# Two output projections of a two-block kernel, from single-precision matmuls to products of high and low parts

## The reference

```python
def first_block(...):
    for layer in range(DEPTH):
        x = x + FFN_HALF * swiglu(rms_norm(x, norm_g[layer, 0]), ffn_w13[layer, 0], ffn_w2[layer, 0])
        h = rms_norm(x, norm_g[layer, 1])
        if layer < N_A_LAYERS:
            y_mix, q_mem = short_conv_mixer(h, conv_w_in[layer], conv_w[layer])
        else:
            ...
            y_mix = causal_mla_attention(q_nope, q_rope, k_nope, k_rope, v)
        y_mem = memory_attention(q_mem, mem, mem_norm_g[layer], w_mem_kv[layer], g_mem_q[layer], g_mem_k[layer])
        x = x + jnp.concatenate([y_mix, y_mem], axis=-1) @ w_out[layer]
        x = x + FFN_HALF * swiglu(rms_norm(x, norm_g[layer, 2]), ffn_w13[layer, 1], ffn_w2[layer, 1])
```

## Time and profile before

| | us |
|---|---|
| median of 3 runs | 3403.96 |
| lowest to highest | 3402.34 to 3404.91 |
| the profiled execution | 3403.58 |
| its span, first to last instruction | 3401.8 |
| mean granted TensorE clock | 0.981 |
| out0 on TensorE | 322.6 to 350.5 |
| out1 on TensorE | 960.0 to 990.9 |

### The profile page before, as it was taken

How to read it: one execution, slowest core, us unless ns; L and a number is a source line. 1 busy time by engine, 2 the same in 40 slices (tenths; PEclk the granted TensorE clock), 3 DMA queues, 4 the chain that set the end, 5 groups by cost and what they waited for, 6 DMA issues and landing times.

```text
span 3401.8 us, 51940 instructions
## 1 busy us (share of the span) xinstructions
PE 3274.9 (96%) x20178; PEld 2934.0 (86%) x20178; DVE 1975.3 (58%) x2057; ACT 1623.6 (48%) x1916; POOL 1248.1 (37%) x507
## 2 busy tenths in 40 slices
PE   7999999999799999999999999997999999999998
PEld 7998999998479989898999898986788888888886
DVE  4544644644434464252443471616888888888887
ACT  4343434332233344531443355403777777777775
POOL 6764787870038855250886353400000000000000
PEclk9999999999699999999999999998999999999999
DMA  5443444543124433344444433344988988988986
GB/s 221 168 160 127 170 180 160 185 176 133 50 101 184 173 137 138 123 161 149 174 184 162 160 126 147 137 149 172 354 332 330 368 329 328 369 329 329 367 330 245
DMA packets 97078, 707.31 MB, mean 208 GB/s; under 512 B 10784, under 2 KB 10784, under 8 KB 10944
## 3 DMA queue, kind: packets, MB, share of 16 engines
q1 hardware_dynamic: 96768, 704.42, 55.5%
q10 hardware_dynamic: 144, 1.05, 0.1%
q0 software_dynamic: 48, 0.13, 0.0%
HBM read 704.51 MB, written 1.05 MB: 207 GB/s over the span
## 4 chain that ended last, share of the span: by engine, by line
PE 84%; DVE 5%; issue 4%; POOL 3%; DMA 2%; ACT 2%; DVEq 0%; POOLq 0%; ACTq 0%; SPq 0%
PE bank L578 20%; PE bank L579 20%; PE bank L580 20%; PE bank L667 10%; POOL half_lo L540 3%; DVE kept L2095 2%; PE bank L664 2%; PE bank L957 2%; DMA ring<-experts 2%; PE bank L1087 1%; PE bank L761 1%; PE bank L1104 1%; PE bank L635 1%; PE bank L783 1%; PE bank L1131 1%
## 5 line engine op out<-in xcount | busy, mean ns | idle before, releaser
L540 POOL TENSOR_TENSOR half_lo<-ring,half_hi 128x1024 fp32r<-128x1024 f32 x502 | 1247.2, 2491 | 967.4 <-ACT half_hi L1213 964.0
L1213 ACT ACTIVATE half_hi<-ring 128x1024 fp32r<-128x1024 f32 x502 | 528.8, 1060 | 759.8 <-PE bank L580 651.3
L578 PE MATMUL bank<-h_hi,half_hi 128*128 128x256 f32 x2928 | 839.1, 287 | 11.2 <-POOL half_lo L540 8.4
L579 PE MATMUL bank<-h_lo,half_hi 128*128 128x256 f32 x2928 | 830.8, 284 | 0.0
L580 PE MATMUL bank<-h_hi,half_lo 128*128 128x256 f32 x2928 | 830.8, 284 | 0.0
L1625 ACT ACTIVATE expert_parts<-ring 128x1024 fp32r<-128x1024 f32 x672 | 674.7, 1054 | 282.5 <-DMA ring<-experts 224.6
L578 PEld LDWEIGHTS bank<-h_hi,half_hi 128*128 128x128 f32 x2928 | 563.5, 192 | 17.5 <-POOL half_lo L540 6.6
L2289 DVE TENSOR_TENSOR expert_parts<-ring,expert_parts 128x1024 fp32r<-128x1024 f32 x448 | 527.6, 1222 | 74.5 <-ACT expert_parts L1625 72.9
L579 PEld LDWEIGHTS bank<-h_lo,half_hi 128*128 128x128 f32 x2928 | 563.4, 192 | 0.7
L580 PEld LDWEIGHTS bank<-h_hi,half_lo 128*128 128x128 f32 x2928 | 563.2, 192 | 0.0
L578 PE MATMUL bank<-expert_parts,h_hi 128*128 128x512 f32 x896 | 360.0, 402 | 11.6 <-DVE kept L2276 6.9
(11 more groups left out here) (299 smaller groups left out, 4397.6 us busy)
## 6 DMA issues: line engine op xcount, KB each, us to landing
ring<-experts SPq DMA_DIRECT2D x336, 1024.0 KB, 4.8
ring<-stream SPq DMA_DIRECT2D x330, 1024.0 KB, 4.8
con<-consts SPq DMA_DIRECT2D x1, 1473.0 KB, 8.2
kept<-x_in SPq DMA_DIRECT2D x1, 1024.0 KB, 4.8
kept<-mem SPq DMA_DIRECT2D x1, 1024.0 KB, 16.3
lent<-mem SPq DMA_DIRECT2D x1, 1024.0 KB, 18.3
lent<-mem ACTq DMA_DIRECT2D x1, 1024.0 KB, 8.0
out<-kept SPq DMA_DIRECT2D x1, 1024.0 KB, 3.9
```

The lines of the kernel that those rows point to most:

```text
L540: nc.gpsimd.tensor_tensor(half_lo[:, h % HALVES, :], ring[:, u % RING, s * HALF:(s + 1) * HALF], half_hi[:, h % HALVES, :].bitcast(F32), A ...
L578: mm(dst, w_hi, x_hi, start=start, stop=False, skip_group_check=shared)
L579: mm(dst, w_hi, x_lo, start=False, stop=False, skip_group_check=shared)
L1213: nc.scalar.activation(half_hi[:, h % HALVES, :], ring[:, u % RING, s * HALF:(s + 1) * HALF], ACT.Copy).then_inc(hi_ready, 1)
```

## The change

out0 and out1 become split units too (`is_parted`), and a new function `parted` on TensorE multiplies them: three fp32r products for each tile, as elsewhere, over each half's four tiles of input channels, both output halves accumulating over the two halves of the unit. Their inputs are no longer one f32 page: VectorE writes each head's result and the gated convolution twice, as a high part (a copy to fp32r) and a low part (the subtraction of the high part). For out0, TensorE's first half waits only for the first two pairs of the convolution (`conv_part`), its second half for everything (`y_ready`). ScalarE makes the halves of out0 and out1 through the same `feed`, and `opening_by_units` now runs `done` for each of the four units.

```diff
--- before
+++ after
@@ -87,6 +87,11 @@
     return name[:3] == "ffn" or name in ("conv_in", "mla_in") or name[:2] in ("xq", "gx", "ax", "ay", "gr", "mu", "mo", "gm")
 
 
+def is_parted(name):
+
+    return is_split(name) or name in ("out0", "out1")
+
+
 def layer_order(l):
 
     runs = [("kv", 0, 8) if l else ("kv", 6, 2), ("mu", 0, 4), ("xq", 0, 4), ("ax", 0, 4), ("gx", 0, 4), ("wv", 0, 1), ("ay", 0, 1),
@@ -121,7 +126,7 @@
         STREAM.append(START[name] + j)
         UNIT_OF.append(name)
 
-SPLIT = [is_split(name) for name in UNIT_OF]
+SPLIT = [is_parted(name) for name in UNIT_OF]
 RANK = [sum(SPLIT[:u]) for u in range(DENSE_UNITS + 1)]
 SPLIT_UNITS = [u for u in range(DENSE_UNITS) if SPLIT[u]]
 
@@ -439,7 +445,6 @@
         mem_raw, mem_n = page(3), (page(5), page(9))
         rs_x, rs_m, rs_xx = rs[:, 4 * TOK:5 * TOK], rs[:, 3 * TOK:4 * TOK], rs[:, 5 * TOK:6 * TOK]
         mem_k, mem_v, mem_q = page(10)[:, 4:6, :], page(10)[:, 6:8, :], page(11)[:, 6:8, :]
-        Y_conv, Y_mla = page(5), page(7)
         gate_c, conv_u, conv_y = page(6, CT), padded(7, CT, 2), page(8, CT)
         k_nope, k_rot, k_rope = page(8)[:, 0:6, :], page(8)[:, 6:7, :], page(8)[:, 7:8, :]
         v_mla = tokens(11, MLA_HEADS * VHD)
@@ -449,6 +454,17 @@
         q_rope, q_rot = page(3)[:, 0:3, :], page(3)[:, 3:6, :]
         rs_flat, sg_flat = rs, sg[:, :, :].rearrange("p a b -> p (a b)")
         mem2 = page(4)
+        def part(i):
+
+            return expert_parts[:, lent_pages.index(i), 0:KT * TOK].rearrange("p (k t) -> p k t", k=KT)
+
+        mem_parts = [hid_hi[:, i, j * TOK:(j + 1) * TOK] for i in range(2) for j in range(2)]
+        conv_hi = [part(5)[:, k, :] for k in range(CT)] + mem_parts[0:2]
+        conv_lo = [part(11)[:, k, :] for k in range(CT)] + mem_parts[2:4]
+        mla_hi = [part(10)[:, k, :] for k in range(6)] + mem_parts[0:2]
+        mla_lo = [hid_lo[:, i, j * TOK:(j + 1) * TOK] for i in range(2) for j in range(2)] \
+            + [part(10)[:, k, :] for k in (6, 7)] + mem_parts[2:4]
+
         xk, xv, xq, gx = page(5), tokens(6, D), page(8), page(10)
         yx, merged = xq, gx
         ax, ay, gr = padded(9, KT, 3), page(7), page(3)
@@ -591,6 +607,26 @@
                         last = products(b[:, m * 256:m * 256 + 256], w_hi[:, cols], w_lo[:, cols], h_hi[:, k, :],
                                         h_lo[:, k, :], k == 0, k == KT - 1)
                     last.then_inc(first_done if m == 0 else unit_done, 1)
+
+            def parted(b, u, x_hi, x_lo, token_major, ready=None):
+
+                for s in range(2):
+                    w_hi, w_lo = half(u, s)
+                    if ready:
+                        ready[s]()
+                    for m in range(2):
+                        dst = b[:, m * 256:(m + 1) * 256]
+                        for i in range(4):
+                            k = 4 * s + i
+                            start, stop = s == 0 and m == 0 and i == 0, s == 1 and i == 3
+                            if token_major:
+                                toks, cols = slice(m * PARTS, (m + 1) * PARTS), slice(i * 256, (i + 1) * 256)
+                                last = products(dst, x_hi[k][:, toks], x_lo[k][:, toks], w_hi[:, cols], w_lo[:, cols],
+                                                start, stop, True)
+                            else:
+                                cols = slice(i * 256 + m * PARTS, i * 256 + (m + 1) * PARTS)
+                                last = products(dst, w_hi[:, cols], w_lo[:, cols], x_hi[k], x_lo[k], start, stop, True)
+                    last.then_inc(first_done if s == 0 else unit_done, 1)
 
             def column_half(b, u, m):
 
@@ -646,13 +682,16 @@
                 opening(*pairs)
                 project(None, units[2:])
 
-            def project(src, units, token_major=False, fresh=False):
+            def project(src, units, token_major=False, fresh=False, parts=None, ready=None):
 
                 for u in units:
                     p = SLOT[u]
                     b = bank[p % 3]
 
                     wait(pe, bank_read[p % 3], p // 3)
+                    if parts:
+                        parted(b, u, parts[0], parts[1], token_major, ready if u == units[0] else None)
+                        continue
                     if SPLIT[u]:
                         split_columns(b, u, 0, fresh and u == units[0])
                         continue
@@ -845,8 +884,9 @@
                           lambda h: project(None, conv[6:7] if h == 0 else []),
                           lambda: project(None, conv[4:5]))
 
-            pe.wait_ge(y_ready, t.add("y", 1))
-            project(Y_conv, AT["out0"])
+            y_all = t.add("y", 1)
+            project(None, AT["out0"], parts=(conv_hi, conv_lo),
+                    ready=(lambda: pe.wait_ge(conv_part, 2), lambda: pe.wait_ge(y_ready, y_all)))
             ffn(AT["ffn01"][0], D_FF // 256)
 
             ffn(AT["ffn10"][0], D_FF // 256, lambda: norm(KT, KT, ones))
@@ -910,7 +950,7 @@
                       lambda h: [(q_nope[:, h, :], k_nope[:, h, :]), (MEM_HALF(q_rot, h), k_rot[64 * (h % 2):64 * (h % 2) + 64, 0, :])],
                       lambda h, j, m: v_mla[:, m, h * VHD:(h + 1) * VHD], 1, VHD)
             pe.wait_ge(y_ready, t.now("y"))
-            project(Y_mla, AT["out1"])
+            project(None, AT["out1"], parts=(mla_hi, mla_lo))
             ffn(AT["ffn11"][0], D_FF // 256)
 
 
@@ -1273,10 +1313,12 @@
                 for j in range(4):
                     x_square(j)
 
-            def opening_by_units(g, u0):
+            def opening_by_units(g, u0, units=None):
 
                 for j in range(4):
-                    if j == 3:
+                    if units:
+                        done(units[j])
+                    elif j == 3:
                         feed(2 * RANK[u0], u0 - 1 + RING)
                     x_high(g, j)
                     x_square(j)
@@ -1390,7 +1432,7 @@
             act.wait_ge(sin_in, 1)
             nc.scalar.activation(angle[:, 1:3, :], angle[:, 1:3, :], ACT.Sin).then_inc(sin_ready, 1)
             t.add("x", 1)
-            opening_by_units(gain("norm_g", 2), AT["ffn01"][0])
+            opening_by_units(gain("norm_g", 2), AT["ffn01"][0], AT["out0"])
             ffn_x(AT["ffn01"][0], D_FF // 256)
             def mem2_squares():
                 act.wait_ge(mem_loaded, 16)
@@ -1470,7 +1512,7 @@
             attention(MEM_HEADS, lambda h: value_out(kv, 1) if h == 0 else None, lambda: value_out(kv, 0))
             attention(MLA_HEADS)
             t.add("x", 1)
-            opening_by_units(gain("norm_g", 5), AT["ffn11"][0])
+            opening_by_units(gain("norm_g", 5), AT["ffn11"][0], AT["out1"])
             ffn_x(AT["ffn11"][0], D_FF // 256)
 
             for l in range(2):
@@ -1904,9 +1946,18 @@
                     last.then_inc(normed, 1)
                     t.add("norm", 1)
 
-            def mem_attention(Y, early=None, between=None):
-                attention(MEM_HEADS, MEM_HD ** -0.5, None, lambda h: v.tensor_copy(
-                    MEM_HALF(Y[:, CT:, :], h), bank[7][64 * (h % 2):64 * (h % 2) + 64, 0:TOK]), early, between)
+            def put_parts(got, hi, lo):
+
+                did(v.tensor_copy(hi, got))
+                return v.tensor_tensor(lo, got, hi.bitcast(F32), ALU.subtract)
+
+            def mem_attention(early=None, between=None):
+
+                def put(h):
+                    r = slice(64 * (h % 2), 64 * (h % 2) + 64)
+                    return put_parts(bank[7][r, 0:TOK], mem_parts[h // 2][r, :], mem_parts[2 + h // 2][r, :])
+
+                attention(MEM_HEADS, MEM_HD ** -0.5, None, put, early, between)
 
 
             def lam_start():
@@ -1966,8 +2017,12 @@
 
                 q = SLOT[conv[7 + j]]
                 dve.wait_ge(unit_done, conv[7 + j] + 1)
-                v.tensor_tensor(Y_conv[:, 2 * j:2 * j + 2, :], two(bank[q % 3]), conv_y[:, 2 * j:2 * j + 2, :],
-                                ALU.mult).then_inc(bank_read[q % 3], 1)
+                pair = slice(2 * j, 2 * j + 2)
+                v.tensor_tensor(conv_y[:, pair, :], two(bank[q % 3]), conv_y[:, pair, :], ALU.mult).then_inc(bank_read[q % 3], 1)
+                wait_read(dve, q)
+                did(v.tensor_copy(part(5)[:, pair, :], conv_y[:, pair, :]))
+                v.tensor_tensor(part(11)[:, pair, :], conv_y[:, pair, :], part(5)[:, pair, :].bitcast(F32), ALU.subtract)\
+                 .then_inc(conv_part, 1)
 
             def beside_head(h):
                 if h == 0:
@@ -1982,7 +2037,7 @@
                 if h == 3:
                     gate_b(1)
 
-            mem_attention(Y_conv, lambda: conv_in(0), beside_head)
+            mem_attention(lambda: conv_in(0), beside_head)
             gate_b(2)
 
             tick(y_ready)
@@ -2062,10 +2117,10 @@
                 else:
                     norm_piece(q_rope, 2 * i - 6, 5 - i, P("g_q_rope"), sg_flat, i == 4)
 
```

(5 more changed lines are left out.)

## The result

| us | before | after |
|---|---|---|
| median (15 runs each) | 3404.82 | 3412.20 |
| lowest to highest | 3401.28 to 3413.94 | 3404.72 to 3426.96 |
| the profiled execution | 3403.58 | 3404.72 |
| its span | 3401.8 | 3402.9 |
| ratio after/before, 95% interval | | 1.0026 [1.0017, 1.0034] |

The kernel became slower by 0.26%, about 8.8 us (5.8 to 11.6). The forecast was 3415 in a range of 3402 to 3421, with 0.71 on slower.

What follows compares the result with a forecast made beforehand. TensorE, busy 96% of the span, and whatever leaves it waiting were taken to set the time. First projection +0.8 us and second +10.8 made +11.6 on 3403.58, 0.4 below the median: 3415, range 3402 to 3421.

Steps and rivals of the forecast that it cites:

- rival A: Loads don't hold ScalarE on the path, taking away 10.4 us and 2.9 of clock terms: 3402 us; chance 0.13.
- B: Rival: a clean gain, neither loads nor GpSimd hold anything, -7.6 us: 3396 us; chance 0.07.
- D: Rival: the three products take as long as the f32 one: 3424 us; chance 0.10 together with C.
- C: Rival: low clock through one more MLA head or longer into out1, +3 to +5 us: 3419; 0.10 with D.
- products of out0, out1: Each of eight units goes from 6.92 to 5.76 us on TensorE: 4.6 us less per projection.
- `gate_b(0)` beside head 2: GpSimd holds VectorE's added cast and subtraction, so head 3's transposes start 3.7 us later; 1.9 by the median row.
- clock behind it: After TensorE's idle time beside `gate_b(0)` the clock falls: 1.7 us more, bounds 0 and 3.5.
- squares of the queries: Before the query norms, ScalarE's out1[0] copies wait for a load behind kv0[3]: 6.3 us later, bounds 2.0 and 9.5.
- first norm round: After 8.4 us idle, the first query norm round runs at half clock, 2.09 for 1.13 us: 0.9 more.
- first `at_t`: In head 0, ScalarE's out1[1] copy waits for a load behind kv0[4]: 4.1 us later, bounds 1.1 and 8.
- kv0[5]: Behind head 0's values, kv0[5] runs at the lower clock: 2.0 us more, bounds 0 and 3.5.
- puts in memory attention, MLA: Each head's copy gets a second VectorE instruction: 0.9 us in the second memory attention, 0.9 in MLA.

Runs made afterwards that it cites:

- e2: Changed kernel with only the first projection (out0) split, the second as before: 3403.24 us, 0.9995 of before.
- e3: Changed kernel with only the second projection (out1) split, the first as before: 3413.59 us, 1.0024 of before.
- e4: Changed kernel, but ScalarE makes out1's first halves later, beside MLA heads 4 and 5: 3400.12 us, 0.9991 of before.
- e7: Changed kernel with both the edits of e5 and e6, later convolution parts and late out1 halves: 3394.83 us, 0.9981 of before.
- e5: Changed kernel, but VectorE makes the gated convolution's parts later, the first pair's beside head 3: 3408.97 us, 1.0018 of before.
- e8: Kernel before plus only two ScalarE waits for out1's loads, behind the read-outs of kv0[3] and kv0[4]: 3412.34 us, 1.0030 of before.
- e1: Changed kernel run again without edit, for a second profile: 3410.80 us, 1.0021 of before.
- e6: As e4, but out1's first half is made beside MLA head 0 and the other two beside head 5: 3397.16 us, 0.9985 of before.

## Why the prediction was right

**The cause.** The forecast rested on ScalarE's copies waiting in order for loads that cannot start before kv0[3] and kv0[4] are done. It is shown from three sides: the loss lies in out1 (e2, e3), it goes when the copies stand elsewhere (e4 -10.7, e7 against e5 -14.1, where the forecast's rival A takes 13.3 away), and it comes without the rest of the change (e8). Rivals A and B fall with this, and D with the 5.67 us of a unit. C, a low clock through one more head, is in neither profile: in after and e1 the clock was back one MLA head earlier than in the profile of before, worth about 3 us, and e8, which has before's products and copies, shows that earlier return too (e2 shows before's later one). The slowest executions, up to 3426.96 us, have no profile, so there C isn't excluded.

**The terms,** as forecast and as the profile of after has them, us:

| term | forecast | after |
|---|---|---|
| products of out0, out1 | -4.6, -4.6 | -4.6, -5.0 |
| start of out0 | -1.2 | -1.2 |
| `gate_b(0)` beside head 2 | +3.7 | +2.1 |
| clock behind it | +1.7 | 0 |
| second half of out0's first unit | +0.9 | +0.7 |
| opening of ffn01 | +0.3 | +0.2 |
| squares of the queries | +6.3 | +6.3 |
| first norm round | +0.9 | +0.9 |
| first `at_t` | +4.1 | +4.1 |
| kv0[5] | +2.0 | +1.6 |
| puts in memory attention, MLA | +0.9, +0.9 | +0.8, +0.9 |

(Each is a difference of two rows: 3.36 - 1.23; the wait of 0.73; 8.32 - 2.06; 8.73 - 7.17 for kv0[5], whose own row of before was at the full clock; 4 x (6.92 - 5.67) for out1.) The rows ahead of out1 add up to 14.6 us where 11.8 were seen. Head 0's values, 1.97 us at the low clock in place of 1.08, are 0.9 more that the forecast left out, and kv0[4] is 0.4 less; the MLA head just named takes the sum back by 3.3. The two large terms are right to a tenth, since slot, order and load time fixed them: the load took 4.26 + 0.6 us from kv0[3]'s end, against the 4.8 assumed.

**What was mis-sized.** The first projection was forecast at +0.8 and measured at -2.7 in the profile (2.3 ahead, from a convolution that began 0.45 late) and at -0.9 in e2. The term that failed is `gate_b(0)`, +3.7. Its alternative of 1.9 was nearer: the cast was held (2.14 us), but the subtraction then won the race by 0.17 us. In e1 neither was held, and TensorE still waited 2.97 us, for the scaling. In e5 a subtraction did lose the race and took 2.90 us. The mechanism is right and which instruction pays is a matter of a tenth of a microsecond. The rule of the Trainium skill (SBUF — State Buffer, Who interferes with whom) that the one to start first keeps the ports agrees with both outcomes: 0.69 us at 0.17 us ahead, with GpSimd's instruction at 2.72 us in place of some 2.40, and 2.90 us at 0.05 us behind.

The clock's fall behind that wait, +1.7, did not come in after: 3.36 us idle were followed by a stretch at 1.00, whereas 2.67 us before head 1 had been followed by 0.50. In e2 it came: after the same 3.36 us the transposes took 1.12 us in place of 0.66. In e7 it came too, after 2.97 us, and in e1, e4, e5 and e6 it did not. So this term is there in some executions and not in others; the forecast had 0 as its lower bound and yet put 1.7 in the sum, which was its weakest step.

**Signs and sums.** The signs named ahead came true: idle times of 4.26 and 4.19 us for loads, 8.32 and 4.77 us on TensorE, 24.2 us for out0, a cast of 2.14 us; only the subtraction, 0.69 us and not "well over 0.7", did not. Neither sign of being wrong came: the squares start 6.8 us behind kv0[3]'s end, and the clock was down between 290 and 350 us (0.57 from 294 to 298). The forecast's own range has a slip: with clock terms of 6.8 in place of 4.6 the sum is 13.8 and its upper end 3417, not 3419. The stated range goes to 3421 for rival C and doesn't rest on it.

**Right by luck in part.** After the 11.6 of the sum the median rose by 7.4 to 8.8 us. Of the difference, 1.7 to 3.5 are the first projection (+0.8 forecast, -0.9 in e2, -2.7 in the profile). The forecast started from a profile of before whose out1 began slowly, and took that as unchanged; the slow start is missing in after, e2 and e3, and there in the other six. So two single profiles can differ by 3.2 us for this alone, and the sum was safer as a difference than as a time.

**Open.** What makes the granted clock fall or return at a given place in one execution and not in the next; why after scatters over 22 us and before over 13; and whether the casts' place (e5, e7 against e6) is worth anything.

## What to carry to other kernels

Before giving units to a prefetch that an in-order engine drives, write down for each unit when its slot comes free and what stands behind the copy in that engine's queue: a prefetch that runs ahead of its data is a barrier. The cheaper products gained 9.6 us, and two places in the order cost more (10.4); with the copies put where the load had landed, the kernel became 4 to 9 us faster than before (e4, e6, e7; the interval of e4 just includes no gain). And take the account from waits that repeat in every execution, since clock-dependent terms can come and go.

## What the runs showed of the hardware

- One code in several executions: VectorE's reciprocal for ffn01, just behind out0, starts at 363.73 us in the profile of before and at 366.5 in e3 and e8, whose code is before's up to there. The 2.8 us go with low-clock stretches at other heads: from 306 to 310 us the granted clock is 0.57 in both, and 1.00 in the profile of before.
- A VectorE cast of 128x512 from SBUF takes 0.43 us alone, 1.17 or 2.14 with a GpSimd subtraction under way, by how much of that is left: it ends 0.3 us behind GpSimd's instruction both times. A scaling of 128x256 twice takes 0.61 us alone (e3), 1.60 (e6) to 2.70 (e4) so, and 4.17 in before at 289.18 us, where two of GpSimd's subtractions follow one another.
- A wait of 8.32 us cost little more clock than one of 2.06 us. Before, the first norm round behind it took 1.13 us and the next ones 2.07; in after all took 2.07, 0.94 us in sum, and the low clock ended at the second MLA head, where before's ended at the third. In e4, behind 2.06 us again, three rounds took 1.13.
